# Up projections of three feed-forward layers by seven block products for eight, down projection in two halves

## The reference, cut to what matters

```python
def half_ffn(x, shift, scale, gate, w_in, w_out, g, b):
    h = modulate(x, shift, scale)
    a, u = jnp.split(h @ w_in, 2, axis=-1)
    y = (jax.nn.silu(a) * u) @ w_out
    return layernorm(ALPHA * x + 0.5 * gate * y, g, b)
```

## Time and profile before

| | before |
|---|---|
| median of 3 runs | 3166.09 us (3165.67 to 3167.77) |
| profiled execution, its own time | 3173.73 us |
| its span | 3171.9 us |
| mean granted TensorE clock | 0.969 of full |
| PE busy | 2999.4 us, 95% |
| DVE busy | 1584.4 us, 50% |
| ACT busy | 842.7 us, 27% |

### The profile page before, as it was taken

How to read it: one execution, slowest core, us unless ns; L and a number is a source line. 1 busy time by engine, 2 the same in 40 slices (tenths; PEclk the granted TensorE clock), 3 DMA queues, 4 the chain that set the end, 5 groups by cost and what they waited for, 6 DMA issues and landing times.

```text
span 3171.9 us, 41843 instructions
## 1 busy us (share of the span) xinstructions
PE 2999.4 (95%) x16423; PEld 2473.8 (78%) x16423; DVE 1584.4 (50%) x2397; ACT 842.7 (27%) x1262; POOL 281.1 (9%) x393
## 2 busy tenths in 40 slices
PE   5999999999976999999999999999996998899997
PEld 2588888887853778888888888888874897688885
DVE  3434343456547364334335634444464888454544
ACT  0411111124244151111112411111144666322221
POOL 1000000010010101000001000000001663000000
PEclk7899999999997999999999999999997999999998
DMA  7344342211121225343431122212112100233330
GB/s 267 118 146 145 119 132 67 62 48 51 53 66 53 60 84 165 118 141 127 145 107 54 54 66 66 62 57 66 55 33 47 28 23 18 67 106 93 93 99 33
DMA packets 292647, 269.31 MB, mean 85 GB/s; under 512 B 31111, under 2 KB 257263, under 8 KB 292432
## 3 DMA queue, kind: packets, MB, share of 16 engines
q1 hardware_dynamic: 269936, 188.95, 19.9%
q0 software_dynamic: 21760, 76.03, 6.8%
q10 hardware_dynamic: 864, 3.15, 0.3%
HBM read 262.85 MB, written 5.24 MB: 85 GB/s over the span
## 4 chain that ended last, share of the span: by engine, by line
PE 90%; DVE 4%; ACT 3%; DMA 1%; issue 1%; POOL 1%; SPq 0%; ACTq 0%; DVEq 0%; POOLq 0%
PE PSALL L2095 24%; PE PSALL L2096 23%; PE PSALL L2097 23%; PE PSALL L2016 2%; PE PSALL L2144 2%; PE PSALL L2145 2%; PE PSALL L2146 2%; PE PSALL L2119 2%; PE PSALL L2524 1%; PE PSALL L2509 1%; PE PSALL L2058 1%; PE PSALL L2405 1%; PE PSALL L2107 1%; PE PSALL L2470 1%; PE PSALL L2472 1%
## 5 line engine op out<-in xcount | busy, mean ns | idle before, releaser
L2095 PE MATMUL PSALL<-HHI,WHIA 128*128 128x512 f32 (+1 forms) x1344 | 466.3, 347 | 6.8 <-DVE HLO L1783 4.3
L2096 PE MATMUL PSALL<-HLO,WHIA 128*128 128x512 f32 (+1 forms) x1344 | 463.8, 345 | 0.0
L2097 PE MATMUL PSALL<-HHI,WLOA 128*128 128x512 f32 (+1 forms) x1344 | 463.4, 345 | 0.0
L1539 DVE SCALAR_TENSOR_TENSOR X<-PSALL,GATE,X 128x512 f32<-128x512 f32 (+1 forms) x568 | 346.6, 634 | 211.5 <-PE PSALL L2097 209.4
L2096 PE MATMUL PSALL<-HLO,WHIB 128*128 128x512 f32 (+1 forms) x1296 | 445.5, 344 | 0.0
L2095 PE MATMUL PSALL<-HHI,WHIB 128*128 128x512 f32 (+1 forms) x1296 | 445.3, 344 | 0.0
L2097 PE MATMUL PSALL<-HHI,WLOB 128*128 128x512 f32 (+1 forms) x1296 | 445.0, 343 | 0.0
L2095 PEld LDWEIGHTS PSALL<-HHI,WHIA 128*128 128x128 f32 x1344 | 255.8, 190 | 45.2 <-issue 9.5
L2097 PEld LDWEIGHTS PSALL<-HHI,WLOA 128*128 128x128 f32 x1344 | 255.5, 190 | 30.6
L2096 PEld LDWEIGHTS PSALL<-HLO,WHIA 128*128 128x128 f32 x1344 | 255.9, 190 | 29.7
L2095 PEld LDWEIGHTS PSALL<-HHI,WHIB 128*128 128x128 f32 x1296 | 245.8, 190 | 28.9
(11 more groups left out here) (292 smaller groups left out, 4934.3 us busy)
## 6 DMA issues: line engine op xcount, KB each, us to landing
RAW<-in_ffn_w_in_dram SPq DMA_DIRECT2D x176, 512.0 KB, 4.2
ADA<-in_ada_w_dram POOLq DMA_DIRECT2D x144, 512.0 KB, 5.1
RAW<-in_ffn_w_out_dram SPq DMA_DIRECT2D x88, 512.0 KB, 3.5
RAW<-in_ev_w_in_dram SPq DMA_DIRECT2D x20, 512.0 KB, 4.1
WRAW<-in_mla_w_q_up_dram SPq DMA_DIRECT2D x16, 288.0 KB, 3.0
RAW<-in_ev_w_out_dram SPq DMA_DIRECT2D x8, 512.0 KB, 4.8
RAW<-in_mla_w_in_dram SPq DMA_DIRECT2D x8, 512.0 KB, 3.8
RAW<-in_mla_w_out_dram SPq DMA_DIRECT2D x8, 512.0 KB, 4.7
```

The source lines that it names most:

```text
L1539: dve.scalar_tensor_tensor(X[:, m, lo:lo + n], down_bank(m, s, S), GATE[:, j, m, s:s + 1], X[:, m, lo:lo + n], ALU.mult, ALU.add).then_inc ...
L2095: te.matmul(out, w_hi, x_hi(k), start=(k == 0), stop=False)
L2096: te.matmul(out, w_hi, x_lo(k), start=False, stop=False)
L2097: x = te.matmul(out, w_lo, x_hi(k), start=False, stop=(k == ks - 1))
```

## The change

In `ffn0`, `ffn1` and `ffn2`, the units A(2) to A(10) and B(2) to B(9), 17 of 22 in each layer, form their up projection as a product of a 2x2 by a 2x2 block matrix with seven block products. The blocks are: gate and up part, by the first four and the last four row blocks of the model width, by the first 384 and the last 384 tokens (`HALF`). Each block product is 4 row blocks by 3 matmuls of 384 columns, 12 matmuls, and a unit has 84 matmuls of 384 columns. The token-side sums (`TM_`, `TH_`, `TL_`, and block 12 of H itself, which is replaced) are made once per layer by DVE and ACT, behind the classic units of iteration 1; block 12 is put back in the last iteration. The weight-side sums are made for every unit, in place in `RAW`, by DVE, and split by both engines into `WSH` and `WSL`. The block products are put together by DVE (`second_sum` to `gate_second`). The units of iterations 0 and 1 and the last B keep the old form (`up_classic`). The down projection of pair i-1 is cut: its first eight groups follow up A(i), its last eight follow up B(i), with its weights loaded by column halves (`rows_load`), and the high part of the gated values is made by ACT (`gate_hi`) and the low part by DVE (`gate_low`) at the head of an iteration. `mod_take` stands between the groups 6 and 7 of the first half on DVE, and PE still waits for `mod_ok` before up B. SP loads in the order of use: both halves of B(i), half of W(i-1), both halves of A(i+1), the other half W(i).

```diff
-        ffn("ffn0", 2, N_ADA - ADA_FIRST, "h0", "ln0")
+        wide("ffn0", N_ADA - ADA_FIRST, "h0", "ln0")
         even_mixer()
-        ffn("ffn1", 2, N_ADA, "ln1", "ln2")
-        ffn("ffn2", 2, 0, "ln2", "ln3")
+        wide("ffn1", N_ADA, "ln1", "ln2")
+        wide("ffn2", 0, "ln2", "ln3")
```

TensorE, new:

```diff
+            def seventh(place, block, bank):
+                out = PS[bank][:, 0:HALF]
+                for k in range(4):
+                    w_hi, w_lo = (t[:, place, P * k:P * k + P] for t in (WSH, WSL))
+                    te.matmul(out, w_hi, hi[block](k), start=(k == 0), stop=False)
+                    te.matmul(out, w_hi, low[block](k), start=False, stop=False)
+                    x = te.matmul(out, w_lo, hi[block](k), start=False, stop=(k == 3))
+                return x
+            def up(slot, i, q, between=None):
...
+                te.wait_ge(mul[slot], p.gs + 2 * i)
+                te.wait_ge(g_lo, 5 * v + 1)
+                seventh(0, "11", b).then_inc(g_pe, 1)
+                te.wait_ge(g_lo, 5 * v + 5)
+                te.wait_ge(t_lo, 10 * blk + 6)
+                seventh(4, "T2", b + 1).then_inc(g_pe, 1)
+                if slot == "B":
+                    te.wait_ge(evac, p.evac + 2 * KC * (i - 1) + KC)
+                seventh(1, "21", b + 2).then_inc(g_pe, 1)
+                if between is not None:
+                    between()
+                te.wait_ge(g_p1, v + 1)
+                seventh(2, "T3", b).then_inc(g_pe, 1)
+                te.wait_ge(g_add, 7 * v + 1)
+                seventh(3, "T1", b + 1).then_inc(g_pe, 1)
+                te.wait_ge(g_add, 7 * v + 2)
+                te.wait_ge(t_lo, 10 * blk + 8)
+                seventh(6, "T4", b + 2).then_inc(pe[slot], 1)
+                te.wait_ge(g_add, 7 * v + 3)
+                te.wait_ge(lo_done, q + 2 + 6 * i)
+                seventh(5, "22", b).then_inc(pe[slot], 1)
...
+            def body(i, ada=False):
+                up("A", i, wide_q(name, "A", 1) - 6, early(i) if ada else None)
+                down(i - 1, range(0, 8), wide_q(name, "W0", 1) + 6 * i - 6 + 1, ada)
+                if ada:
+                    te.wait_ge(mod_ok, p.ada + i)
+                up("B", i, wide_q(name, "B", 1))
+                down(i - 1, range(8, 16), wide_q(name, "W1", 1) + 6 * i + 1,
+                     taken=lambda: te.wait_ge(g_add, 7 * seven(name, "B", i) + 6))
```

VectorE, the order of one unit, of the loop body and of the last iteration, new (sums and `gated_` work on 384 columns; `low_first` and `split_lo` on 1024; the other weight operations on 512; `block12_mix` is three dependent operations of 768 and `block12_low` one):

```diff
+            def unit(slot, i, q, rows, groups, bias=None):
...
+                second_sum(slot, i)
+                rows()
+                gate_first(slot, i)
+                low_first()
+                third_sum(slot, i)
+                difference()
+                fourth_sum(slot, i)
+                up_second(slot, i)
+                total()
+                low_difference()
+                up_first(slot, i)
+                low_total()
+                gated_first(slot, i)
+                low_second()
+                gate_second(slot, i)
+                mix_second()
+                last_mix()
+                gated_second(slot, i)
+                for e in groups[:2]:
+                    accumulate(i - 1, e)
+                low_third()
+                for e in groups[2:4]:
+                    accumulate(i - 1, e)
+                low_last()
+                for e in groups[4:7]:
+                    accumulate(i - 1, e)
+                if bias:
+                    bias()
+                accumulate(i - 1, groups[7])
...
+            up_second("A", last)
+            if tables is not None:
+                tables()
+            up_first("A", last)
+            gated_first("A", last)
+            block12_mix(0, slice(0, 2), 1, ALU.add, 18)
+            gate_second("A", last)
+            block12_low(0, 9)
+            gated_second("A", last)
+            q = wide_q(name, "B", last)
+            split_lo("B", 0, q, last)
+            accumulate(last - 1, 0)
+            accumulate(last - 1, 1)
+            block12_mix(1, slice(2, 4), 1, ALU.add, 21)
+            accumulate(last - 1, 2)
+            accumulate(last - 1, 3)
+            block12_low(1, 10)
+            for e in range(4, 7):
+                accumulate(last - 1, e)
+            split_lo("B", 1, q + 1, last)
+            for e in range(7, 16):
+                accumulate(last - 1, e)
```

ScalarE, one unit and the last iteration, new:

```diff
+            def unit(slot, i, rows, q, ada=False):
...
+                first_copy(slot, i)
+                rows()
+                silu_first(slot, i)
+                raw_hi(n, q, i, (g_pe, 5 * v + 3))
+                mix_hi(n, 1, 2, first, 0, (g_pe, 5 * v + 4)).then_inc(g_hi, 1)
+                mix_hi(n, 2, 3, second, 0, (g_pe, 5 * v + 5)).then_inc(g_hi, 1)
+                second_hi(n, q, i, (pe[slot], used + 1))
+                silu_second(slot, i)
+                mix_hi(n, 3, 4, second, 1, (g_pe, 5 * v + 2)).then_inc(g_hi, 1)
+                if ada:
+                    ada_take(p.ada + i - 1)
+                mix_hi(n, 4, 5, first, 1, (pe[slot], used + 2)).then_inc(hi_done, 2)
...
+            silu_second("A", last)
+            q = wide_q(name, "B", last)
+            split_hi("B", 0, q, last, p.B + 2 * last)
+            for k in range(2):
+                block12_hi(k, 18 + 3 * k + 3)
```

More of the change, by code:

```diff
@@ L451, in build, with wide_q, seven, blocks_of @@
         CONV_END.append((CONV_END[-1] if n else 0) + (4 if kind == "rg" else 4 if 8 <= c else 3))
+    UNITS = 2 * (FI - 2) - 1
+    BLOCKS = {"ffn0": 0, "ffn1": 1, "ffn2": 2}
+    def wide_q(name, kind, i):
+        q = plan[name].q
+        if isinstance(i, int) and i == 0:
+            return q + {"B": 2, "A": 4, "W0": 6}[kind]
+        if isinstance(i, int) and i == FI - 1:
+            return q + 6 * i + {"W1": 1, "B": 2, "W0": 4, "W1L": 5}[kind] - 6 * i
+        return q + {"B": 1, "W1": 3, "A": 4, "W0": 6}[kind]
+    def seven(name, slot, i):
+        return UNITS * BLOCKS[name] + 2 * (i - 2) + "AB".index(slot)
+    def blocks_of(part):
+        H = (HHI, HLO)[part]
+        T = (TH_, TL_)[part]
+        return {"11": lambda k: H[:, k, 0:HALF], "21": lambda k: H[:, 4 + k, 0:HALF], "22": lambda k: H[:, 4 + k, HALF:TOK],
+                "T4": lambda k: H[:, k, HALF:TOK], "T1": lambda k: T[1][k // 2][:, k % 2, :],
+                "T2": lambda k: T[2][k // 2][:, k % 2, :], "T3": lambda k: T[3][k // 2][:, k % 2, :]}
     def down_groups(S):
@@ L560, in ffn, with wide, unit_load, rows_load @@
             body(FI - 1, last=True)
-        ffn("ffn0", A["ffn_w_in"][0, 0], A["ffn_w_out"][0, 0])
+        def wide(name, w_in, w_out):
+            def unit_load(slot, u, q, i=0):
+                for half in range(2):
+                    ffn_load(w_in, w_out, slot, u, half, q + half, i)
+            def rows_load(half, u, q, i=0):
+                sp.wait_ge(lo_done, q - 1 + 6 * i)
+                sp.dma_start(RAW[raw_slot(q)][:, :].rearrange("p (c n) -> p c n", c=2),
+                             w_out.rearrange("(u c p) n -> p u c n", c=2, p=P)[:, bass.ds(u, 1), :, 512 * half:512 * half + 512]
+                             .squeeze(1)).then_inc(raw_in[raw_slot(q)], 16)
+            unit_load("A", 0, plan[name].q)
+            unit_load("B", 0, wide_q(name, "B", 0))
+            unit_load("A", 1, wide_q(name, "A", 0))
+            rows_load(0, 0, wide_q(name, "W0", 0))
+            with sp.Fori(1, FI - 1) as i:
+                unit_load("B", i, wide_q(name, "B", i), i)
+                rows_load(1, i - 1, wide_q(name, "W1", i), i)
+                unit_load("A", i + 1, wide_q(name, "A", i), i)
+                rows_load(0, i, wide_q(name, "W0", i), i)
+            last = FI - 1
+            rows_load(1, last - 1, wide_q(name, "W1", last), last)
+            unit_load("B", last, wide_q(name, "B", last), last)
+            rows_load(0, last, wide_q(name, "W0", last), last)
+            rows_load(1, last, wide_q(name, "W1L", last), last)
+        wide("ffn0", A["ffn_w_in"][0, 0], A["ffn_w_out"][0, 0])
         def proj_load(w, chunk, q):
@@ L1628, in tables @@
             co_wait()
-        ffn("ffn0", 2, 0, N_ADA - ADA_FIRST, ADA_FIRST, "ln0", "ev_in", lambda: tables(0))
+        wide("ffn0", 0, N_ADA - ADA_FIRST, ADA_FIRST, "ln0", "ev_in", lambda: tables(0))
         ln_end("ln0", 2)
@@ L1847, in _ @@
         residual("ln1", 2, 2)
-        ffn("ffn1", 2, 2, N_ADA, N_ADA, "ln2", "ffn2", lambda: tables(1))
+        wide("ffn1", 2, N_ADA, N_ADA, "ln2", "ffn2", lambda: tables(1))
         ln_end("ln2", 2)
         residual("ln2", 2, 3)
-        ffn("ffn2", 2, 3, 0, 0, "ln3", "mla_in")
+        wide("ffn2", 3, 0, 0, "ln3", "mla_in")
         ln_end("ln3", 2)
```

480 lines of the change are left out of this document (475 added, 5 removed).

## The result

The change made the kernel 1.5% faster. Four executions of the changed kernel took 3118.26, 3119.98, 3122.10 and 3123.00 us, median 3121.04; the kernel before took 3166.93 in the same comparison. The ratio of the two is 0.9853, with a 95% interval of 0.9836 to 0.9870, so 41 to 52 us were gained. The forecast was 3112.0 us in a range of 3088 to 3142: inside the range, and 9 us too low.

What follows compares the result with a forecast made beforehand. PE was taken as the bound, busy 100.00 of 100 us in the third layer's loop. -106.4 + 15.0 + 20.3 + 13.2 + 4 (clock) = -53.9 us against 3173.73, scaled to the median: 3112 us, range 3088 to 3142.

Steps and rivals of the forecast that it cites:

- 51 units: Units with block products: up plus its matmuls 14.57 us after for 16.66 before, 2.09 less each, -106.4 us.
- mod_ok: PE's wait before up B in 6 + 9 ada iterations: 1.0 us each, +15.0 us.
- last iterations, with their clock: Late down groups behind DVE's chain: 6.1, 7.5 and 6.7 us, +20.3; clock 1 us at each such place.
- first iterations, with their clock: PE waiting for DVE and ACT: 8.6 us in the third layer, 2.3 in each other, +13.2; clock 1 us.
- The pace: Matmuls of 384 columns put at 173.5 ns, on the line between 256 and 512 columns; bounds 170.5 and 179.6.
- Rival D: 384-column matmuls keep the per-column pace of 256, 179.6 ns: +26 us, 3138; chance 0.05.
- What DVE gets: DVE's chain in a steady unit, first eviction ending at 18.1 to 18.3 us, hidden behind PE by 0.2 us.
- rivals A: DVE's 14 overlaps are gone, chain 1.19 us longer, each unit waits 0.95: +48 us, 3160; chance 0.10.
- B: DVE becomes the bound, each overlap a 0.08 delay, chain 2.3 us longer: +107 us, 3219; chance 0.06.
- Rival C: Weights land late, up to 5.0 us, and each unit waits some 0.5: +25 us, 3137; chance 0.05.
- Rival E: Code fetched again in the loops, 2.6 us a turn, 1.5 idle; 24 turns some 22 us, 3134; chance 0.02.
- The scaling: Sum of -53.9 us taken against the profiled execution's 3173.73, 0.24% above the median 3166.09, scaled to 3112.

Runs made afterwards that it cites:

- experiment 1: Changed kernel with PE's wait for mod_ok moved from ahead of the first block product of B to ahead of the second, in the loops' ada iterations; 3110.03 us.
- experiment 7: Changed kernel with the seventh block product done twice in each unit, 12 matmuls of 384 columns more; 3215.05 us.
- experiment 4: Changed kernel with up_second and low_difference done twice on DVE in every unit, each second one behind the first by a semaphore; 3159.59 us.
- experiment 6: Changed kernel with the edits of experiment 1 and experiment 2 together; 3088.92 us, ratio to the kernel before 0.9749.
- experiment 2: Changed kernel with DVE's order in the last iterations changed: tables ahead of third_sum, two evictions ahead of gated_second, others between mixes and splits; 3104.68 us.
- experiment 10: Changed kernel with TH and TL still the moving operand but holding one plain block each, the subtractions replaced by a maximum; 3126.00 us.
- experiment 5: Changed kernel with one extra DVE operation of 128 columns ahead of up_second in every unit, up_second behind it by a semaphore; 3125.98 us.

## Why the prediction was right, point by point

| term | predicted | measured | from |
|---|---|---|---|
| 51 units | -106.4 | -99.5 | 51 x (25.02 - 23.07) |
| mod_ok | +15.0 | +14.5 | 15 x 0.97, experiment 1 |
| last iterations, with their clock | +20.3, +3 | +20.3 | 114.6 - 3 x 31.45 |
| first iterations, with their clock | +13.2, +1 | +17.0 | what is left of 47.7 |
| sum | -53.9 | -47.7 | the three layers |

**The pace.** 173.5 ns was right for the operands that had been in the trace: P0, P2, P5 and P6 take 2.080 to 2.087 us, 173.3 to 173.9 ns a matmul, and the repeated product of experiment 7 173.6. The mis-sized step is that all seven products were given this price, 2.082 us. P1, P3 and P4 take their moving operand from new tiles and 2.120 us each, 0.115 us more in a unit, and the rest of the 0.14 is the hundredths of the others and of down. Rival D, the whole unit at 179.6 ns, is out: the mean was 175.0.

**What DVE gets.** The chain was followed to a tenth: `gate_first` 6.45 and 6.49, `low_first` 8.56 and 8.59, the first eviction's end 18.1 and 18.11. The cover came out as 0.6 us and not 0.2, for three reasons, all in the step from that end to group 4. The landing of the weights added nothing in a steady unit, where 0.2 was put in. The handing over to PE cost 0.15, where 0.04 and 0.19 were put in. And group 4 starts at 18.89 and not at 18.74, because the products are slower. 0.2 + 0.2 + 0.08 + 0.15 gives 0.63. Experiment 4 confirms the sizes behind it: 1.32 us more in the chain became 0.70 in the unit. By this the rivals A (1.19 longer) and B (2.3 longer) would have cost some 0.6 and 1.7 us in a unit; that they did not occur is seen in the rows, where an operation with three waits of its own, `third_sum`, starts at 1910.27 while `low_first` ends at 1910.35. The overlap of 0.08 us stays. The Trainium skill, page "VectorE: DVE Perf Modes", section "The DRAIN you can't avoid", says that the next operation does not start before the pipe is empty, and also that one that is not held starts earlier. The prediction used the first half alone; the rows here agree with the second, by these 0.08 us.

**Rival C**, weights late, is out in the steady units: `difference` waited for the load in 5 of 51 units, 5.3 us in all. But 2.17 and 2.41 of them are in one place, A(2) of the first and of the second layer, and there rival C is what happened. The second layer:

```profile
1225.93 0.69 DVE L1949 TENSOR_TENSOR RAW<-RAW,RAW 128x512 f32<-128x512 f32 x1 [2.41 <-DMA RAW<-in_ffn_w_in_dram]
```

```profile
1233.88 0.50 PE L2677 MATMUL PSALL<-GHIA,WHIW 128*128 128x512 f32 x1 [1.57 <-DVE X L1872]
```

In A(2) of the first layer this load took 5.7 us to land, with the DMA engines 0.98 busy from 228 to 232, among loads of ada; in the loop of the third layer the median is 4.0. The two waits move together from run to run: 2.7 and 1.8 us in the first layer of experiment 1, 1.9 and 1.0 in that of experiment 6, 1.6 and 0.8 in that of experiment 2. No run changed the load alone. **Rival E**, code fetched again (24 turns at 2.6 - 1.5 us would be 26 and not 22, and no run shows the 2.6): the instruction queue q8 has 3 packets and q14 one in the 375 us from 1815 to 2190 with the eight turns of the third layer's loop, and all units in them are 23.07 or 23.08 us long. The Trainium skill, page "Runtime: NRT & Kernel Launch", section "Instruction fetch mechanics", names the case; no run here shows a stall of that kind.

**mod_ok.** Named with its place and size, and experiment 1 shows the cause.

**Last iterations.** The mechanism was right (the chain there runs through `block12_mix`, ACT's 1024 columns, `block12_low`, `split_lo` to the first eviction, as the chain in order of time of the second layer has it):

```profile
1641.79 0.41 issue
1642.20 1.04 ACT WHIB L955
1643.24 0.74 ACT HHI L1100
1643.98 0.02 issue
1644.01 0.96 DVE HLO L2070
1644.96 0.47 DVE GMA L1933
1645.43 1.14 DVE WLOB L1564
1646.57 0.67 DVE X L1872
```

The waits were smaller, 14.3 us for 20.3 (gaps of 4.67, 5.50, 4.07 and 0.61 between starts, less the pace of 0.12 and 0.23), and the clock cost more: 20.3 - 14.3 = 6.0 us in three places against 1 us each. The two errors nearly cancel. For the third layer the wait was put at 4.2 with 1.6 and 0.3 behind it; it was 3.95 with 0.4, as the later groups found their evictions done while PE ran at half speed. If the half-speed matmuls only took the place of the later waits, DVE's chain sets the sum either way; that is argued here, and shown only for A(2) below.

**First iterations.** The sum of the third layer was right: 54.4 us for 50.04 in the first, and 51.66 for 46.15 in the second, +9.8 against 9.6. Its terms were not all. Behind the first wait (2.8 for 2.5) PE lost another 1.4 us at half speed, in a place where the prediction counted no clock. Inside A(2) the wait for `P` was 3.4 for 4.0, and the one of 2.1 at group 4 is 0.2: 1.6 us of half-speed matmuls fill the rest, and group 4 starts at 1827.01, 0.05 behind the end of the eviction it needs. That is shown from the other side too: in experiment 6 PE keeps full clock behind the same wait for `P` and then waits 1.5 us at group 4, and A(2) with its half of down takes 28.58 us there and 28.59 here. The chain on DVE sets the time, and the clock costs nothing on top of it.

The two other layers, put at 2.3 each, cost 3.3 and 3.5 (54.76 and 55.04 us from up A(2) to up A(3) for 51.50 in the next iterations; the 0.4 us that is missing to the table's 17.0 lies in hundredths elsewhere). The longer ada iteration does shorten the wait for `P`, from 3.4 to 1.6. What the prediction had at nothing there is the late landing of weights (rival C), with 1.6 and 1.9.

**The scaling.** The sum belonged to the profiled execution of before, 3173.73, and gives 3119.8, near the 3118.26 of the profiled execution after. But 6.5 us of these 3173.73 were the head of that execution at half clock, which the one after did not have. So the agreement of these two is luck: 6.2 us too much gain in the layers, 7.8 us of head and rest. Against the medians the error is 9 us, 6.2 of them the terms above, and 3 within what the interval leaves.

## What to carry to other kernels

When arithmetic is moved from the bounding engine to one that is half idle, the steady loop can be had nearly for free, as here 99.5 us with a cover of 0.6 us; what is lost is lost at the one wait for `mod_ok` and in the first and last iterations, 52 us here, and more than half of it was order (experiment 6 takes 32 off): place the other engine's work in the first and last iterations by the time at which each result is wanted. Put a wait on a semaphore ahead of the first instruction that touches the shared thing, not ahead of the block that contains it: one product later was worth 11 us. And before one more product is taken out, lengthen the other engine's chain by a known amount: it tells the cover, and here it told that a further product would be worth 0.6 us and not 2.1.

## What the runs showed of the hardware that was not expected

- Where the moving operand of a matmul lies can change its pace: 384 columns took 176.7 ns from TH and TL and 173.3 to 173.9 from HHI and HLO, in the units of the third layer's loop, and experiment 10 shows the same 176.7 with other contents.
- A gap in PE's work is not always answered by the clock. The same gap of 3.8 us between the starts, in A(2) of the third layer, in the changed kernel and in experiment 5:

```profile
1812.00:1816.00 4.00, 3.38 (x11) 3.39 (x12) 3.52 (x5) 1.96 (x5) 0.00 (x0) 0.57 0.00 0
```

```profile
1818.00:1822.00 4.00, 3.31 (x19) 3.32 (x20) 3.59 (x5) 1.96 (x4) 0.00 (x0) 1.00 0.00 0
```

  At 0.57, near 1.2 GHz, PE did 11 matmuls, at full clock 19. In the first execution group 4 then started 0.33 us behind the matmul before it, almost without a wait; in the second, whose chain is 0.33 us longer, the starts there lie 2.09 us apart, and the clock fell behind that wait.
- Shorter waits than these were answered too: behind the 2.8 us in the first iteration of the third layer the clock was 0.50 from 1772 to 1774, and behind 2.5 us in experiment 4 it was 0.58 and 0.57.
- A matmul that waited started 0.05 us after the end of the operation that released it, its weight load was recorded behind the same wait, and the next matmul came 0.10 us late.
- The granted clock can stay at half while PE is busy: before the first product with H, PE was busy for 10.00 of 10 us at 0.50 in the profile of before, and the head of the program took 6.5 us longer than in that of the changed kernel.
